# Gates of 16 of the 96 groups of one-hot expert matrices multiplied on GpSimd in place of ScalarE, in a two-block decoder kernel

## What is computed

```python
s = einsum('chpd,hpnd->chpn', q, keys); sv, si = top_k(s, 16)
cand = sv[:, :, 0, :, None] + sv[:, :, 1, None, :]
top_s, sel = top_k(cand.reshape(C, 8, 256), 16)
eidx = take_along_axis(si0 * 128 + si1, sel)
g = softmax(top_s)
act = gelu(einsum('chkd,cd->chk', u_tab[eidx], xb))
out = einsum('chk,chkd->cd', g * act, v_tab[eidx])
```

## Time and profile before

| | |
|---|---|
| median of 3 runs | 2103.89 us (2101.98 to 2104.72) |
| the profiled execution | 2109.07 us, its span 2107.3 us |
| TensorE busy | 2063.9 us, 98% of the span |
| VectorE busy | 1439.7 us, 68% |
| ScalarE busy | 1001.8 us, 48% |
| GpSimd busy | 1031.7 us, 49% |
| mean granted clock of TensorE | 0.994 of full speed |
| chain that ended last | TensorE 92%, VectorE 4% |

### The profile page before, as it was taken

One profiled execution on the slowest core, in us unless ns is written; L12 is line 12 of the kernel. 1 busy time (PEld: TensorE's weight loads), 2 busy tenths in 40 slices (PEclk: granted clock), 3 DMA queues, 4 the chain that ended last, 5 costly groups with the idle time before them and its releaser, 6 DMA issues.

```text
span 2107.3 us, 31668 instructions
## 1 busy us (share of the span) xinstructions
PE 2063.9 (98%) x11809; PEld 1854.4 (88%) x11809; DVE 1439.7 (68%) x2810; ACT 1001.8 (48%) x1829; POOL 1031.7 (49%) x584
## 2 busy tenths in 40 slices
PE   8998999999999999999999999999999999999998
PEld 7745789999999999999999999999977777877777
DVE  5237458849997847878878788887687636057763
ACT  4236333358888843333333333333556652256642
POOL 3213345555455666666566766564344444411242
PEclk9999999999999999999999999999999999999999
DMA  5230124456778899999999999997322222310021
GB/s 200 79 98 11 61 90 147 162 182 254 257 262 294 317 346 330 346 332 357 321 328 357 337 339 341 344 343 246 98 93 70 91 90 100 101 49 31 21 81 60
DMA packets 145623, 419.67 MB, mean 199 GB/s; under 512 B 13504, under 2 KB 60224, under 8 KB 143680
## 3 DMA queue, kind: packets, MB, share of 16 engines
q1 hardware_dynamic: 108608, 283.42, 39.1%
q0 software_dynamic: 36864, 134.23, 17.1%
HBM read 375.06 MB, written 42.53 MB: 198 GB/s over the span
## 4 chain that ended last, share of the span: by engine, by line
PE 92%; DVE 4%; issue 1%; ACT 1%; DMA 1%; POOL 0%; SPq 0%; DVEq 0%; ACTq 0%
PE bank L488 24%; PE bank L489 24%; PE bank L490 24%; PE bank L866 4%; PE bank L1065 2%; PE bank L655 1%; PE wide L1088 1%; PE wide L1076 1%; PE bank L1088 1%; PE wide L613 1%; PE bank L749 1%; PE bank L751 1%; PE bank L750 1%; DMA wraw<-in_wstream 1%; PE wide L508 1%
## 5 line engine op out<-in xcount | busy, mean ns | idle before, releaser
L2563 POOL TENSOR_TENSOR wl<-wraw,wh 128x1024 fp32r<-128x1024 f32 x273 | 683.3, 2506 | 776.7 <-ACT wh L1244 776.5
L488 PE MATMUL bank<-XH,wh 128*128 128x384 f32 (+2 forms) x1552 | 545.5, 351 | 6.5 <-DVE tmp L2383 2.9
L489 PE MATMUL bank<-XL,wh 128*128 128x384 f32 (+2 forms) x1552 | 539.1, 347 | 0.0
L490 PE MATMUL bank<-XH,wl 128*128 128x384 f32 (+2 forms) x1552 | 536.2, 345 | 0.0
L1244 ACT CAST wh<-wraw 128x1024 fp32r<-128x1024 f32 x362 | 378.5, 1046 | 206.9 <-PE bank L490 172.0
L488 PE MATMUL bank<-WTH,wh 128*128 128x384 f32 x1024 | 343.1, 335 | 1.1 <-issue 0.9
L490 PE MATMUL bank<-WTH,wl 128*128 128x384 f32 x1024 | 342.7, 335 | 0.0
L489 PE MATMUL bank<-WTL,wh 128*128 128x384 f32 x1024 | 342.4, 334 | 0.0
L488 PEld LDWEIGHTS bank<-XH,wh 128*128 128x128 f32 x1552 | 291.4, 188 | 30.7 <-issue 9.7
L489 PEld LDWEIGHTS bank<-XL,wh 128*128 128x128 f32 x1552 | 291.6, 188 | 18.3 <-issue 1.9
L490 PEld LDWEIGHTS bank<-XH,wl 128*128 128x128 f32 x1552 | 292.5, 188 | 16.3
(11 more groups left out here) (528 smaller groups left out, 3339.9 us busy)
## 6 DMA issues: line engine op xcount, KB each, us to landing
wraw<-in_wstream SPq DMA_DIRECT2D x362, 512.0 KB, 4.4
g_scratch<-gs SPq DMA_DIRECT2D x12, 2048.0 KB, 7.4
gr<-g_scratch SPq DMA_DIRECT2D x15, 1536.0 KB, 13.1
a_scratch<-tmp SPq DMA_DIRECT2D x72, 192.0 KB, 2.1
tmp<-a_scratch SPq DMA_DIRECT2D x46, 192.0 KB, 7.1
sq<-a_scratch SPq DMA_DIRECT2D x26, 192.0 KB, 8.7
shifted<-hc_scratch SPq DMA_DIRECT2D x12, 270.0 KB, 4.8
h<-in_hT SPq DMA_DIRECT2D x8, 264.0 KB, 6.7
```

Source lines behind the costliest of these rows:

```text
L488: pe.matmul(o, w1, x1, start=n == 0, stop=False)
L489: pe.matmul(o, w1, x2, start=False, stop=False)
L490: m = pe.matmul(o, w2, x1, start=False, stop=n == len(ks) - 1)
L2563: return pool.tensor_tensor(lo, src, hi.bitcast(F32), ALU.subtract)
```

## The change

For 16 groups, listed in `POOL_GATED`, the four gate products on ScalarE are left out. GpSimd multiplies the first one-hot matrices of all four tokens by their gates in one instruction of 128x512, in place, with the gate read as a broadcast; it does so in its own `scatter`. It waits for `hot`, the signal of VectorE, and tells a new semaphore, `hot_gate_pool`, for which TensorE waits once per group in place of once per token.

```diff
--- before.py
+++ after.py
@@ -380,6 +380,7 @@
     qp_made, key_mm, routed, gate_exp = signal("qp_made"), signal("key_mm"), signal("routed"), signal("gate_exp")
     ijg_mm, ijg_made = signal("ijg_mm"), signal("ijg_made")
     hot, hot_gate, iota_out = signal("hot"), signal("hot_gate"), signal("iota_out")
+    hot_gate_pool = signal("hot_gate_pool")
     scat_mm, scat_out = signal("scat_mm"), signal("scat_out")
     gelued = signal("gelued")
 
@@ -428,6 +429,8 @@
     def q_of(m):
 
         return sq[0][:, 0:512] if m == 0 else rb[:, 0:512] if m == 1 else qT[:, m, :]
+
+    POOL_GATED = (0, 1, 30, 31, 32, 33, 48, 49, 62, 63, 64, 65, 74, 75, 84, 85)
 
     def hots_at(t0):
 
@@ -861,8 +864,11 @@
         def scatter(t0):
             for q in range(t0 // 4, t0 // 4 + 2):
                 bank = next_bank(("scat", q), (scat_out, q))
+                if q in POOL_GATED:
+                    pe.wait_ge(*hot_gate_pool.at(q))
                 for i in range(4):
-                    pe.wait_ge(*hot_gate.at(4 * q + i))
+                    if q not in POOL_GATED:
+                        pe.wait_ge(*hot_gate.at(4 * q + i))
                     mm = pe.matmul(bank[:, i * 128:i * 128 + 128], hots[q % 4][1][:, i, :], hots[q % 4][0][:, i, :],
                                    start=True, stop=True, skip_group_check=True)
                 mm.then_inc(*scat_mm.tell(q))
@@ -1466,6 +1472,8 @@
         def scatter(t0):
             blk = t0 // 32
             def gate(q):
+                if q in POOL_GATED:
+                    return
                 act.wait_ge(*hot.at(q))
                 for t in range(4 * q, 4 * q + 4):
                     act.mul(hots[q % 4][0][:, t % 4, :], hots[q % 4][0][:, t % 4, :],
@@ -2654,7 +2662,11 @@
                 yield
 
         def scatter(t0):
-            pass
+            for q in hots_at(t0):
+                if q in POOL_GATED:
+                    gates_of = ijgT[:, 2, 4 * q:4 * q + 4].unsqueeze(2).to_broadcast([128, 4, 128])
+                    pool.wait_ge(*hot.at(q))
+                    pool.tensor_tensor(hots[q % 4][0], hots[q % 4][0], gates_of, ALU.mult).then_inc(*hot_gate_pool.tell(q))
 
         spilled = [0]
```

## The result

The changed kernel takes **2112.88 us** in the median of 7 runs (2110.39 to 2120.17) against 2104.72 in 7 runs of the kernel before (2101.98 to 2108.02). The ratio is 1.0042, with a 95% interval of 1.0033 to 1.0052: slower by 8 to 9 us, just outside my range. The range was laid on the 2103.89 of the first three runs, which is 0.8 us under the median of all seven; laid on 2104.72 it would have ended at 2113.3. So the edge tells little. What tells is the size: I had added 3.9 us, and 8.2 came. The profiled execution took 2112.88 us too, its span 2111.1.

A forecast was written before the change was run, and what follows sets the result against it. TensorE was taken as the bound, busy 98%, losing 11 us to ScalarE's gates in six turns without a product. Late GpSimd gates there summed to +3.9 us on the median 2103.89: 2107.8 us, range 2103.5 to 2112.5.

The forecast's parts named there:

- the lock: VectorE operations with two SBUF inputs and GpSimd instructions reading SBUF exclude each other, first one going first; assumed for the new products.
- the price of a product: One new 128x512 gate product on GpSimd was taken at 1.04 us, with 1.27 us kept for the range.
- rival 2: The GpSimd product is dear, 1.27 us each: 3.7 us more, 2111.5 us, or 2114 with late fetched rows; chance 0.2.
- rival 1: New products and VectorE's row operations pass each other without blocking: sum 0.0, 2103.9 us, not slower; chance 0.16.
- E: Scatter-stage turn without a product, groups 74 and 75: forecast +0.1 us, or +1.3 if VectorE's row operation wins.
- Rival 3: GpSimd is free when the groups are made: all 11 us come back at most, 2093 us, half 2098; chance 0.07.
- The late rows: Row fetches delayed 2.1 us behind each pair of products, costed at nothing; otherwise 1 to 2 us at two places.
- A: Scatter-stage turn without a product, groups 0 and 1, behind two splits in a row: forecast +0.8 us.
- B: Scatter-stage turn without a product, groups 32 and 33, with groups 30 and 31 gated one turn ahead: forecast +0.75 us.
- F: Scatter-stage turn without a product, groups 84 and 85; VectorE's waiting row operation goes before the pair: forecast +1.2 us.
- C: Scatter-stage turn without a product, groups 48 and 49: row operation over when split begins, +0.1 us; if they meet, +0.9.
- D: Scatter-stage turn without a product, groups 64 and 65, said to repeat the pattern of B: forecast +0.9 us.

## Why the prediction was wrong

**What held.** The direction, the late gates behind the split, the lock and the price of a product. The instructions of the new line, least/median/most in ns:

```profile
L2669 POOL TENSOR_TENSOR hots<-hots,ijgT x10: 1029/1042/2025, 446.6 to 701.1; 128x512 f32<-128x512 f32 x10
L2669 POOL TENSOR_TENSOR below_XL<-below_XL,ijgT x3: 1050/2019/2022, 538.1 to 671.5; 128x512 f32<-128x512 f32 x3
L2669 POOL TENSOR_TENSOR sq<-sq,ijgT x3: 1037/1037/1052, 540.0 to 672.5; 128x512 f32<-128x512 f32 x3
```

1.04 us as taken from the earlier trace rows, so rival 2 falls; that 2112.88 lies within its 2111.5 to 2114 is chance. The Trainium skill (GPSIMD Engine Reference, Performance versus the Vector engine) gives about 2.6 cycles per element, an estimate of 1.11 us; the measured 1.04 decides.

The lock held for the new products, so rival 1 falls: they take 1.04 or 2.02 us and little between. The one at 634.68 starts within VectorE's row operation, and at E the order is turned: GpSimd's second product runs first, and VectorE's row operation takes 2.06 us in place of 1.21:

```profile
634.48 1.33 DVE L2225 SCALAR_TENSOR_TENSOR fetched<-fetched,below_XH 128x1024 f32<-128x1024 f32 x1
...
672.59 2.06 DVE L2225 SCALAR_TENSOR_TENSOR fetched<-fetched,below_XH 128x1024 f32<-128x1024 f32 x1
```

That is the rule of the Trainium skill (SBUF — State Buffer, Who interferes with whom), and the trace agrees, now for products with a broadcast operand too. Rival 3 fell for the reason given: the split ends too late in all six. Times such as it put in reach (2098, at most 2093) came only with another order. The late rows that I cost at nothing did cost nothing that the trace shows: VectorE waits 7.5 us for fetched rows in place of 5.8, but TensorE has no wait for VectorE in the list above.

**Where the sum was short.** A, B, E and F came within 0.25 us of their forecasts, as the table shows. C did not: I let the row operation be over when the split begins, since VectorE would have moved ahead by more than 1 us. It started 0.26 us ahead of the split (590.22 and 590.48), as before (0.25), and the split took 3.17. VectorE could not keep a lead. It makes group q only once TensorE has multiplied group q - 4. The 1.97 us of waiting for ijgT are gone, but ahead of groups 36 and 37 it now waits 1.69 us for TensorE, late at B itself, where it had not waited:

```profile
547.11 2.35 DVE L2193 TENSOR_TENSOR hots<-wide,ijgT 128x1024 f32<-128x1024 f32 x2 [1.69 <-PE bank L872]
```

All its making of groups in `hots` between 440 and 740 us (busy, mean ns, then the idle time before it and what ended it):

```profile
L2193 DVE TENSOR_TENSOR hots<-wide,ijgT 128x1024 f32<-128x1024 f32 x48 | 56.5, 1215 | 18.1 <-PE bank L872 11.7 <-ACT ijgT L1469 6.4
```

(before, the waits for TensorE in this group were 4.7). My own bracket, "If they still meet: +0.9", was right at 0.95; by the sign that I had set (no more than 0.3 us later than the sums) the reading of C was wrong. D did not repeat B's pattern either: its second product is locked out by a row operation at 641.92, so the pair takes 3.02 us where B's took 2.04. I had +0.9; without a drop of the clock (in the kernel that kept TensorE busy and in the one with the longer wait alike) D loses 13.08 - 11.39 = 1.7 us, and F 6.37 - 5.24 = 1.1. The sum of the waits is so 0.97 + 0.71 + 0.95 + 1.7 + 0.15 + 1.1 = 5.6, in place of 3.9. With every lock counted I had 5.9, so this alone would have stayed in my range.

So one step that failed is the sum of the waits, 1.7 us short by C and D. **The step that failed with nothing set against it** is the one before these: "So TensorE takes up its next work 0.10 + 0.82 = 0.92 us after the second product of a pair ends", and behind it "I let it stand undiminished at the end". It takes for granted that TensorE comes out of a wait of over 2 us at the pace at which it went in. No term of the sum and no rival had its clock. In the profiled execution this cost 3.1 us (the stage with and without the two drops). In the median it can only be estimated, from the granted clocks of all executions: 68 runs of the kernel before have a mean of 0.9965, the changed kernel's seven 0.9951, and within the 68 the time rises by about 1.5 us for each 0.001 less. That makes 2.1 us. With the waits' 5.6 it is 7.7 of the 8.2 found. The executions at a clock of 0.997 say from the other side that most of the loss is not the clock: 2103.7 us before (median of 24), 2110.39 to 2111.99 after (3), which is 6.7 us at the least, 1.1 more than the waits. So the clock's share of the median stays an estimate of 1 to 3 us, and no experiment has won it back.

The Trainium skill (TensorE: Matmul & The Clock Gate, Part 1) has TensorE's clock at either of two levels according to how busy the engine has lately been, and says that the number of slow matmuls varies between runs of one kernel. The traces agree on the levels: only 1.00, 0.50 and mixtures of them in a slice. The executions agree on the second: the mean is 0.991 to 0.997 over the changed kernel's seven. That such waits could make the change dearer was there to be weighed, and I didn't weigh it.

## What to carry to other kernels

Where an engine takes over work with a deadline, its place in that engine's program matters more than the engine's idle share: GpSimd was half idle in every version, and a 2.4 us split ahead of the gates made the difference between 2110.5 and 2095.4 us. An idle time of TensorE has two prices, its length and what the clock may lose behind it, so several waits lengthened from 1.1 to over 2 us can cost more than their sum. And where a producer waits for its consumer's buffers, don't count on a lead that it gains at one place: here it was gone before the next, and the collision with a third engine was back.

## What the hardware did that I had not expected

How often a drop of the clock followed, over TensorE's idle times in this stage in the twelve profiled executions (the waits of 1.07 us and less in the kernel before drew none):

| TensorE's idle time | of them | 0.50 during it or right behind |
|---|---|---|
| 1.4 to 1.7 us | 7 | none |
| 2.0 to 2.6 us | 19 | 7 |
| 3.4 to 3.8 us | 3 | 3 |

A drop cost 1.7 us in most stretches and 3.4 in the worst (672 to 684 us with the longer wait). The same wait with the same work around it (2.1 us at B) kept the clock in one kernel and lost it in another, so a single trace can't show whether such a wait is safe. Drops in stages that the change doesn't touch (164 to 176 us above) are part of what spreads the runs of the kernel before from 2102 to 2112 us, by the 1.5 us for each 0.001 of the mean clock; the mean clock alone doesn't fix the time (30 runs at 0.996 take 2104.2 to 2110.8).
